# A hybrid encoder step on one core: residual adds of the second token group done by TensorE instead of VectorE

## What is computed

```
x = x + mix,   mix = concat(gated short conv, Mamba-2 SSD) @ w_out        on rmsnorm(x)
x = x + cross_attn(rmsnorm(x), k, v)                                       ends in @ w_mo
x = x + peer(rmsnorm(x))       8 heads, top 16 of 128x128 experts each, rows of u_tab and v_tab
y = rmsnorm(x, final_norm_w)
```

## Time and profile before

| | |
|---|---|
| median of 3 runs | 1743.04 us (1737.89 to 1744.2) |
| the profiled execution | 1739.22 us, span 1737.3 us |
| PE busy | 1657.5 us, 95% |
| DVE busy | 1165.6 us, 67% |
| ACT busy | 383.8 us, 22% |
| POOL busy | 688.1 us, 40% |
| DMA | 552.62 MB, 318 GB/s over the span |
| mean granted TensorE clock | 0.977 |

### The profile page before, as it was taken

How to read it: one execution, slowest core, us unless ns; L and a number is a source line. 1 busy time by engine, 2 the same in 40 slices (tenths; PEclk the granted TensorE clock), 3 DMA queues, 4 the chain that set the end, 5 groups by cost and what they waited for, 6 DMA issues and landing times. The chain is left out here.

```text
span 1737.3 us, 19883 instructions
## 1 busy us (share of the span) xinstructions
PE 1657.5 (95%) x6994; PEld 1227.9 (71%) x6994; DVE 1165.6 (67%) x2590; ACT 383.8 (22%) x940; POOL 688.1 (40%) x603
## 2 busy tenths in 40 slices
PE   7999999999979998999899999999999999899997
PEld 6888888877756786878876666666666666566643
DVE  2352112788898777869968988776666666766676
ACT  1151123134301276635720002001000000000101
POOL 1000000224334547405655665555444545645542
PEclk9999999999889998999999999999999999999999
DMA  6634534866659969967999999999999999999997
GB/s 202 191 100 136 184 98 156 284 225 214 240 196 353 377 231 395 366 216 254 360 356 404 409 409 409 409 409 409 410 408 409 408 405 407 387 410 410 410 396 272
DMA packets 224338, 552.62 MB, mean 318 GB/s; under 512 B 15696, under 2 KB 112080, under 8 KB 223600
## 3 DMA queue, kind: packets, MB, share of 16 engines
q0 software_dynamic: 82944, 302.03, 45.2%
q1 hardware_dynamic: 118304, 237.69, 37.2%
q10 hardware_dynamic: 22992, 11.64, 2.3%
HBM read 534.22 MB, written 16.42 MB: 317 GB/s over the span
## 5 line engine op out<-in xcount | busy, mean ns | idle before, releaser
L829 POOL DMA_INDIRECT M<-in_u_tab,IDX x288 | 338.4, 1175 | 679.4 <-DVE PEER L1804 332.7
L836 POOL DMA_INDIRECT M<-in_v_tab,IDX x288 | 345.2, 1198 | 344.8 <-DVE X L1825 262.9
L1119 PE MATMUL PSB<-XN,M 128*128 128x256 f32 x2048 | 466.8, 382 | 9.9 <-ACT M L1341 5.2
L1119 PEld LDWEIGHTS PSB<-XN,M 128*128 128x128 f32 x2048 | 391.5, 192 | 110.3 <-issue 54.2
L1127 PE MATMUL PSB<-M,HST 128*128 128x512 f32 x1024 | 459.1, 593 | 4.1 <-DMA M<-in_v_tab 2.8
L1804 DVE CUSTOM_DVE_ANT_0 M<-M,XN 128x1024 f32<-128x1024 f32 x288 | 351.5, 1221 | 132.6 <-DMA M<-in_u_tab,IDX 131.7
L1825 DVE SCALAR_TENSOR_TENSOR X<-M,PEER,X 128x1024 f32<-128x1024 f32 x256 | 327.9, 1281 | 90.9 <-DMA M<-in_v_tab,IDX 87.9
L878 PE MATMUL PSB<-M 128*128 128x256 f32 (+1 forms) x1536 | 362.1, 396 | 6.0 <-DVE M L1435 5.3
L878 PEld LDWEIGHTS PSB<-M 128*128 128x128 f32 x1536 | 293.5, 193 | 65.8 <-DVE M L1435 6.1
L1127 PEld LDWEIGHTS PSB<-M,HST 128*128 128x128 f32 x1024 | 193.4, 190 | 207.0 <-issue 188.8
L885 PE MATMUL PSB<-M 128*128 128x256 f32 (+1 forms) x928 | 214.5, 391 | 6.4 <-issue 3.3
(11 more groups left out here) (222 smaller groups left out, 1042.2 us busy)
## 6 DMA issues: line engine op xcount, KB each, us to landing
M<-in_u_blocks SPq DMA_DIRECT2D x128, 512.0 KB, 6.8
M<-in_v_tab SPq DMA_DIRECT2D x128, 512.0 KB, 6.8
M<-in_w_in SPq DMA_DIRECT2D x24, 1024.0 KB, 6.0
M<-in_w_pq SPq DMA_DIRECT2D x16, 1024.0 KB, 8.6
gate_spill<-M ACTq DMA_DIRECT2D x11, 1024.0 KB, 14.9
M<-gate_spill SPq DMA_DIRECT2D x16, 704.0 KB, 9.4
M<-in_w_out SPq DMA_DIRECT2D x8, 1024.0 KB, 5.0
M<-in_w_mq SPq DMA_DIRECT2D x8, 1024.0 KB, 7.3
```

The lines of the kernel that those rows point to most:

```text
L829: pool.indirect_dma_start(out=UA[:, s % RR, :], out_offset=None, in_=utab, in_offset=bass.IndirectOffsetOnAxis(ap=IDX[:, n:n + 1], axis=0) ...
L836: pool.indirect_dma_start(out=VA[:, s % RR, :], out_offset=None, in_=vtab, in_offset=bass.IndirectOffsetOnAxis(ap=IDX[:, n:n + 1], axis=0) ...
L1119: last = pe.matmul(PSB[:, 4 + b % 2, 0:2 * P], UBLK[:, b % SR, c, :], XN[:, 1:3, c * P:(c + 1) * P], start=(c == 0), stop=(c == DC - 1))
```

## The change

Four edits. (1) `jobs_of` gives the banks of the second group's `o` and `mo` jobs to ScalarE. (2) `token_major` takes a further operand: the 256 columns of the tile's own rows in `X`, which it adds to the same bank as a ninth product with the identity matrix. (3) ScalarE copies the bank to `X`; VectorE does nothing for these jobs. (4) The planner counts no VectorE time for them; its TensorE time stays 3.8 us a job. The first group is untouched.

```diff
-        t_dve = max(t_dve, t_pe - 10) + dve_us(w)
+        t_dve = max(t_dve, t_pe - 10) + dve_us(w) * (w[:2] not in (("o", 1), ("mo", 1)))
...
     if k == "gb" and seg not in SMALL:
+        return [(seg, "A")]
+    if k in ("o", "mo") and seg[1] == 1:
         return [(seg, "A")]
...
-            def token_major(key, w, n, lhs):
+            def token_major(key, w, n, lhs, rest=None):

                 b = open_job(key)
                 for c in range(DC):
-                    last = pe.matmul(b[0:n, 0:BW], lhs(c), w[:, c, :], start=(c == 0), stop=(c == DC - 1))
+                    last = pe.matmul(b[0:n, 0:BW], lhs(c), w[:, c, :], start=(c == 0), stop=(c == DC - 1 and rest is None))
+                if rest is not None:
+                    last = pe.matmul(b[0:n, 0:BW], ident[0:n, 0:n], rest, start=False, stop=True)
                 done(last)
+
+            def own_rows(g, q, t):
+                return X[0:rows(t), t, q * BW:(q + 1) * BW] if g == 1 else None
...
                 token_major(("o", g, q, t), use_block("w_out", BW * q, g), rows(t),
-                            lambda c: GB[:, c, loc(t, 2)] if c < 4 else YBT[:, c - 4, loc(t)])
+                            lambda c: GB[:, c, loc(t, 2)] if c < 4 else YBT[:, c - 4, loc(t)], own_rows(g, q, t))
...
-                token_major(("mo", g, q, t), use_block("w_mo", BW * q, g), rows(t), lambda c: QTg[g][:, c, loc(t)])
+                token_major(("mo", g, q, t), use_block("w_mo", BW * q, g), rows(t), lambda c: QTg[g][:, c, loc(t)], own_rows(g, q, t))
...
+            def rows_back(kind):
+                def drain(g, q, t):
+                    if g == 1:
+                        n = rows(t)
+                        drained(act.copy(X[0:n, t, q * BW:(q + 1) * BW], begin((kind, g, q, t))[0:n, 0:BW]))
+                return drain
...
             def residual(kind):
                 def add(g, q, t):
+                    if g == 1:
+                        return
                     n = rows(t)
```

More of the change, by code:

```diff
@@ L1400, in _ @@
             act.activation(PSM[:, 0:1], EPSC[:, :], ACT.Sqrt)
-            does = {"norm": norm, "turn": turn, "memr": memr, "in": in_, "dt": dt, "cs": cs, "z": z, "kv": kv, "s1": s1, "s2": s2, "s4n": s4n,
+            does = {"norm": norm, "turn": turn, "memr": memr, "in": in_, "dt": dt, "cs": cs, "z": z, "kv": kv, "s1": s1, "s2": s2, "s4n": s4n, "o": rows_back("o"), "mo": rows_back("mo"),
                     "q": q_, "a1": a1, "a2p": a2p, "a2": a2, "pq": pq, "sc": sc,
```

## The result

The kernel after takes 1759.9 us (median of 4 runs, 1757.1 to 1769.1), the kernel before beside it 1740.9 us (4 runs). The ratio is 1.011 with a 95% interval of 1.0085 to 1.0134: 19 us, or 1.1%, slower. I had forecast 1747.4 us, within 0.5% of before, with a range up to 1756. Both the time and the side are missed.

What follows compares the result with a forecast made beforehand. TensorE's delivery of the last scores was taken to set the block stretch's start and the kernel's end. 10.4 - 1.7 - 1.0 - 2.0 - 1.3 = +4.4 us on the 1743.0 us median gave 1747.4 us, range 1736 to 1756.

Steps and rivals of the forecast that it cites:

- The ninth product, +10.4 us: TensorE, second group's `o` and `mo` jobs: 24 added products at 0.432 us each, +10.4 us at full clock.
- The wait and the cold clock in the `o` stretch, -2.7 us: TensorE's 2.45 us wait for VectorE's scaling at 516.04 us swallows 1.7 us; less low clock behind it gives 1.0.
- The norm behind the `o` jobs, "stays": Norm after the last `o` product: one copy takes the place of one add, so the delay added before it stays.
- The wait for the late gather, middle of 0 and -3.9: TensorE's 3.88 us one-hot wait at 662.8 us swallows between 0 and 3.9 us of added products; taken as -2.0.
- The wait at `turn` 2.3, -1.3 us: TensorE's 3.91 us wait at 684.4 us for tile 3's scaled rows swallows the three last ninth products, -1.3 us.
- The sum, +4.4 us at `lk(0)`: Added products less swallowed time: `lk(0)`, `vd(0)` and the end all come 4.4 us later.
- The copy on ScalarE. I take nothing: ScalarE, `o` and `mo` stretches: copies of 0.369 us fit idle time; cost at most 4.4 us, taken as nothing.
- the add that leaves VectorE: VectorE loses 24 adds, 10.1 us; worth nothing by itself after 694 us, since VectorE waits there anyway.
- The planner, "no slot moves over `lk(0)`": Planner fills 10.8 us of freed model time with about 8 slots; none moves from behind `lk(0)` to before it.
- Freed time comes out as longer waits for scores: VectorE's waits for scores before `lk(0)` grow from 15.4 us towards 25 us.
- The distance between `lk(0)` and `vd(0)` stays near 124 us: Start of the block stretch: `lk(0)` and `vd(0)` both start 4 us later, their distance staying near 124 us.
- the gathers collide: Rival: eight gathers come sooner, one or two more late ones reach TensorE; 1753 to 1759 us, chance 0.08.

Runs made afterwards that it cites:

- g1: The changed kernel with a third staging place for chunk 2 and chunk 4's spill issued later, at gate batch 20: 1754.2 us, ratio 1.0071.
- p1: The kernel before with spilled gates laid out in DRAM by token chunk (8 KB spill runs, 512-byte reading runs): 1780.6 us, ratio 1.0231.
- p2: The changed kernel with spilled gates laid out in DRAM by token chunk (8 KB spill runs, 512-byte reading runs): 1793.1 us, ratio 1.0302.
- e1: The changed kernel with the old order of work put back; ninth product and ScalarE's copies stay: 1757.0 us, ratio 1.0086.
- f3: The changed kernel in the old order (ninth product, ScalarE's copies) with a third staging place for chunk 2: 1748.4 us, ratio 1.0033.
- e3: The changed kernel with VectorE instead of ScalarE copying the sums; ninth product and new order stay: 1757.4 us, ratio 1.0095.
- e4: The kernel before with the ninth product alone: old order, VectorE copies the sums instead of adding: 1747.3 us, ratio 1.0041.
- g4: The ninth product with VectorE's copies in the old order, with a third staging place for chunk 2: 1747.6 us, ratio 1.0040.
- f1: The kernel before with a third staging place for chunk 2 of the gate spill: 1742.8 us, ratio 1.0003.
- h3: The changed kernel with the spills of chunks 2 to 7 left out (gates of 96 tokens wrong): 1767.1 us, ratio 1.0139.
- h2: The change in the old order (ninth product, ScalarE's copies) with the spills of chunks 2 to 7 left out: 1762.5 us, ratio 1.0110.
- g2: The kernel of g1 with transpose tt.1 and one-hot batches 0 and 1 of tile 1 back in their old places: 1752.8 us, ratio 1.0064.
- g3: The kernel of f2 with SyncE holding back the first w_pq block until chunk 2's spill has landed: 1754.8 us, ratio 1.0080.
- f2: The changed kernel with a third staging place for chunk 2 and nothing else: 1764.8 us, ratio 1.0128.

## Why the prediction failed, step by step

What after loses, by the ratios: 7 us product with its waits, nothing for ScalarE's copies as such, 5 us new order, 7 us spill (19 of after against 12 of g1 and 12 between p1 and p2). In the old order the spill costs 9 us (e1 against f3), and that is clear of its error of 5 us; the 5 and the 7 are about as large as theirs.

- *The ninth product, +10.4 us:* right, 0.43 us each. (The figure for a bf16 product beside it is not contradicted by these rows: no product here is bf16. It does not carry over to fp32.)
- *The wait and the cold clock in the `o` stretch, -2.7 us:* right. From the first `o` job to `o` of `q` 3, tile 4, 11 products lie, 4.8 us. The first starts 2.3 us later than in before, the last 4.1: 1.8 us were added and 3.0 swallowed.
- *The norm behind the `o` jobs, "stays":* wrong by 1 us. Counted from the last `o` job, profiles with ScalarE's copy gain 1.7 us of delay up to `turn` 1.4 (after, e1, f3), those with VectorE's 0.5 to 0.6 (e3, e4, g4). ScalarE has to make the copy for tile 4 at 552.99 us before the squares of tile 3.
- *The wait for the late gather, middle of 0 and -3.9:* in after it went wholly (wait 3.88 to none), and so it did in e4 and g4. But the DMA engines stayed as full, and in the kernels with ScalarE's copies it was the spill that was late.
- *The wait at `turn` 2.3, -1.3 us:* wrong in sign. It grew from 3.91 to 6.04 us in f3 and 5.8 in g4, with no spill in play. Its chain starts with rows of `X` that come from TensorE itself, so it moves with the load and swallows none of it; why it grew by 2 us besides is open.
- *The sum, +4.4 us at `lk(0)`:* for the product alone it holds roughly. e4's profile has +3.3, but its `o` stretch had started 3.0 us sooner; counted from there it is +6.3, and +2.9 in g4 against f1. e4 is 7 us over before by the ratio, 5.3 by the medians.
- *"The copy on ScalarE. I take nothing", at most 4.4 us:* **this is the step that failed.** The copy's own price is indeed nothing (f3 against g4). The bound was wrong: in the old order the copies brought 8 us (e1 against e4), through a wait of 12.34 us that e4 does not have. The bound counted how long 12 copies last, and not what stood in ScalarE's queue in front of them: a wait for a place that a DMA had to empty. I looked at what the copies would hold up, and at one wait ahead of the SSD norm. I didn't look at the waits that the `gb` copies have in the code. There the place of chunk 2 stands, with 11 us to spare in before. And I took the add that leaves VectorE to be worth nothing or a gain; I did not ask what it would do to the gathers, and with them to the spill.
- *The planner, "no slot moves over `lk(0)`":* true, and not enough; for the order within the dense part the sum has no term. `lk(0)` and all after it are laid out alike in both. But the order moved batches within the dense part, ahead of `q` 7 and ahead of the norms of tiles 3 and 4. That costs 5 us by itself (h3 against h2), and it brings the spill of chunk 4 in front of those norms. A wait of 0.49 us ahead of `a1` 2 became 2.8.
- *"Freed time comes out as longer waits for scores", 15.4 towards 25 us:* only 18.8 in after. *"The distance between `lk(0)` and `vd(0)` stays near 124 us":* it is 119.9 in after (923.2 - 803.4), and why it shrank is open.
- *The rival "the gathers collide"* was the right family with the wrong victim. I priced a late gather at 6 us, at 0.08. What was late was the transfer with the smallest packets, by 13 us. The time ends just above this rival's 1753 to 1759 us, by another way.

What stays open. Why 5 us of the new order are lost in h3: 2.3 us appear in its trace at `a1` 2 and 1.3 more at the transpose behind it, but g2, which takes these batches back, gains only 1 us, within its error. What holds GpSimd's issues in the kernels in which VectorE empties the banks. And the last `vd` but one: from its start to the last one's it is 5.7 us in before, 8.3 in f1, and 10 to 12 in after, e1 and f3, but also 9.3 in e4 and only 6.2 in g4 and 7.5 in g1, so it follows no part of the change. I ran nothing on it.

## What to carry to other kernels

Before work is put on a queue that "has time", list what that queue waits for, DMAs above all, with the time to spare of each wait in the trace. The price of a copy there is the longest wait that can turn up ahead of it or behind it, not the copy's length. Taking work off an engine changes what it lets through: here the gathers came denser, and another transfer paid. Where three streams share full DMA engines, count packets, not bytes. And a part of a change is run alone only if the rest of the program still fits it: an order made for one division of labour, run with another, measures something else.

## What the runs showed of the hardware

- Full DMA engines served three queues packet for packet (1177, 1177, 1179 in 15 us), at 3.6, 1.0 and 0.5 KB a packet. From issue to the last packet the same 1 MB spill took 13.6 us with the gathers held back (before), 32.0 with all three (after), 22.0 with the weights held back (g3), 9.8 in 8 KB runs (p2).
- The issue of a DMA is not always 0.37 us. With two spills of 2064 packets under way the third held ScalarE 11.77 us (f2), with one of them under way 4.22 us (g3); with 8 KB runs each of these issues took 0.33 us (p2).
- The issue of a gather on GpSimd took 7.04 us at one point of the plan and 3.57 at the next where VectorE empties the banks (before), and at most 2.4 us between 600 and 700 us with ScalarE's copies.
- Reading 704 KB in 512-byte runs where 5.6 KB runs had been took 20.4 us instead of 9.4, and cost 40 us over 16 groups, most of it in the block stretch, whose DMA share is 1.02 in before.
